# Up block 0 of the next group computed ahead of the down blocks, and seven block products in 120 chunks instead of 78

## The reference

```
h = rmsnorm(x, norm_mix[l]);  proj = h @ w_in[l]
o_a = dsa_branch(...);  o_b = swa_branch(...)          # both add a relative-position bias
merged = sigmoid(h Wg_A) * (o_a @ w_branch_a[l]) + sigmoid(h Wg_B) * (o_b @ w_branch_b[l])
x = x + merged @ w_out[l]
h = rmsnorm(x, norm_mlp[l])
x = x + jnp.square(jax.nn.relu(h @ w_up[l])) @ w_down[l]
```

## Time and profile before

| | |
|---|---|
| median of three runs | 2711.16 us |
| the profiled execution | 2718.1 us, its span 2716.4 us |
| PE busy | 2696.5 us, 99% of the span, 12756 instructions |
| DVE busy | 1768.3 us, 65% |
| ACT busy | 1365.0 us, 50% |
| DMA queue q1 (weights, spread, moved) | 568.67 MB, 64% of 16 engines |
| granted TensorE clock, mean | 0.998 of full speed |

### The profile page before, as it was taken

The page is one execution under the profiler, slowest core; times in us unless marked ns, Lnnn a source line. Parts: engine busy times, 40 slices in busy tenths (PEclk is TensorE's granted clock), DMA queues, the critical chain, the costliest instruction groups (busy, mean ns, idle before and its releaser), DMA issues.

```text
span 2716.4 us, 35283 instructions
## 1 busy us (share of the span) xinstructions
PE 2696.5 (99%) x12756; PEld 2212.7 (81%) x12756; DVE 1768.3 (65%) x2538; ACT 1365.0 (50%) x1735; POOL 21.0 (1%) x29
## 2 busy tenths in 40 slices
PE   9999999999999999999999999999999999999998
PEld 7788778888888887888887887788888888888886
DVE  5565555556686785876656655555666957769665
ACT  5445554445554555545445455544455545455443
POOL 0000000000000000000000000000000000000000
PEclk9999999999999999999999999999999999999999
DMA  7875545676766666667666655566776666676664
GB/s 240 249 229 164 185 155 186 219 230 232 235 215 210 228 199 229 205 218 238 225 219 217 212 171 179 160 202 219 229 251 230 199 223 222 203 231 210 216 226 154
DMA packets 189697, 574.76 MB, mean 212 GB/s; under 512 B 21432, under 2 KB 56856, under 8 KB 189408
## 3 DMA queue, kind: packets, MB, share of 16 engines
q1 hardware_dynamic: 188000, 568.67, 64.0%
q0 software_dynamic: 1152, 3.80, 0.7%
q10 hardware_dynamic: 384, 0.11, 0.0%
HBM read 533.57 MB, written 38.93 MB: 211 GB/s over the span
## 4 chain that ended last, share of the span: by engine, by line
PE 94%; DMA 2%; DVE 1%; issue 1%; ACT 0%; SPq 0%; ACTq 0%; POOLq 0%; POOL 0%; DVEq 0%
PE acc L444 28%; PE acc L445 28%; PE acc L446 28%; DMA scratch<-spread 1%; PE acc L412 1%; PE acc L413 1%; PE acc L414 1%; PE att L412 1%; PE att L414 1%; PE att L413 1%; DMA moved<-scratch 1%; PE turn L413 0%; PE turn L414 0%; PE turn L412 0%; PE att L502 0%
## 5 line engine op out<-in xcount | busy, mean ns | idle before, releaser
L1095 DVE TENSOR_TENSOR w_lo<-raw,w_hi 128x1024 fp32r<-128x1024 f32 (+1 forms) x866 | 1040.9, 1213 | 598.0 <-ACT w_hi L742 596.3
L742 ACT ACTIVATE w_hi<-raw 128x1024 fp32r<-128x1024 f32 (+1 forms) x866 | 903.3, 1051 | 747.3 <-PE acc L446 688.4
L444 PE MATMUL acc<-w_hi,h_hl 128*128 128x512 f32 x2176 | 866.9, 398 | 2.6 <-DVE w_lo L1095 2.1
L446 PE MATMUL acc<-w_hi,h_hl 128*128 128x512 f32 x2176 | 859.3, 395 | 0.0
L445 PE MATMUL acc<-w_lo,h_hl 128*128 128x512 f32 x2176 | 859.1, 395 | 0.0
L444 PEld LDWEIGHTS acc<-w_hi,h_hl 128*128 128x128 f32 x2176 | 409.9, 188 | 105.2 <-DVE w_lo L1095 5.7
L446 PEld LDWEIGHTS acc<-w_hi,h_hl 128*128 128x128 f32 x2176 | 409.8, 188 | 96.9
L445 PEld LDWEIGHTS acc<-w_lo,h_hl 128*128 128x128 f32 x2176 | 410.1, 188 | 94.1
L444 PE MATMUL acc<-w_hi,o_hl 128*128 128x512 f32 x1064 | 421.5, 396 | 0.3 <-DVE o_hl L1193 0.2
L445 PE MATMUL acc<-w_lo,o_hl 128*128 128x512 f32 x1064 | 420.0, 395 | 0.0
L446 PE MATMUL acc<-w_hi,o_hl 128*128 128x512 f32 x1064 | 419.8, 395 | 0.0
(11 more groups left out here) (215 smaller groups left out, 2155.7 us busy)
## 6 DMA issues: line engine op xcount, KB each, us to landing
raw<-in_w_main SPq DMA_DIRECT2D x928, 512.0 KB, 4.2
scratch<-spread SPq DMA_DIRECT2D x67, 512.0 KB, 2.7
moved<-scratch SPq DMA_DIRECT2D x268, 128.0 KB, 3.4
raw<-in_w_misc SPq DMA_DIRECT2D x16, 336.0 KB, 4.8
xs<-in_x SPq DMA_DIRECT2D x4, 512.0 KB, 7.2
out<-xs SPq DMA_DIRECT2D x8, 256.0 KB, 3.1
bias_b<-bias_rows POOLq DMA_DIRECT2D x4, 384.0 KB, 8.2
bias_rows<-probs POOLq DMA_DIRECT2D x2, 576.0 KB, 10.8
```

The source lines that it names most:

```text
L444: nc.tensor.matmul(o, a_hi, hi[:, kk], start=(k == 0), stop=False)
L446: last = nc.tensor.matmul(o, a_lo, hi[:, kk], start=False, stop=fin)
L742: nc.scalar.activation(w_hi[s][:, 0:2 * width], raw[r][:, 0:2 * width], ACT.Copy).then_inc(hi_ready, 1)
L1095: nc.vector.tensor_tensor(w_lo[s][:, 0:2 * width], raw[r][:, 0:2 * width], w_hi[s][:, 0:2 * width].bitcast(F32), ALU.subtract).then_inc(lo ...
```

## The change

1. **Order in the MLP.** Up units 0 and 1 stand ahead of the loop. The loop now runs over U2, U3, V0, D0, D1, D2, D3, V1, where V0 and V1 are up units 0 and 1 of the next group. V0's block of u waits in `moved` until D3 is done.
2. **Seven products in up units.** Chunks 1, 3, 5 of U2 and of V0 (`WIDE_UP`), and of the last group's U2. Of the down chunks 13 in each looped group stay, in D0 at chunks 3 and 7 instead of 1 and 3. That makes 19 a loop turn and 60 a layer, 120 in all. The up form needs sums of blocks of h, made in three of the four `out` units (`sums_of_h`, `h_sums`, kept in `s_hh`).
3. **How such an up block is taken.** ScalarE copies half of one side bank to `stage` (`take_side`), VectorE makes the sum in five operations (`add_up_sides`), at chunk 3; relu and square follow out of `stage`, and the transpose into `spread` comes at chunk 4, behind the split of chunk 3.
4. **Moved blocks later.** `u_moved` and its sums come at chunks 1 and 2 of the next unit instead of chunks 6 and 7 (V0's at chunks 3 and 4 of V1).
5. **Bias.** `COPIES` 8 instead of 32: one store of 288 KB, then 16 reads of 64 KB (`bias_a`) and 16 of 96 KB (`bias_b`), waited for in pairs. `s_hh` has the room of `bias_b`, so `bias_b` is read again for layer 1, during the last group of layer 0.

```diff
-COPIES = 32
+COPIES = 8
-WIDE = ((1, 3), (1, 3, 5, 7), (1, 3, 5), (1, 3, 5, 7))
+WIDE_UP = ((1, 3, 5), (), (1, 3, 5), ())
+WIDE = ((3, 7), (1, 3, 5, 7), (1, 3, 5), (1, 3, 5, 7))
@@ SyncE
-                    for n in range(1, NBLK):
-                        load_up(g, n)
+                    load_up(g, 2, pass_on(l, E_U + 1, g))
+                    load_up(g, 3, pass_on(l, E_U + 2, g))
+                    load_unit(l, g * 64 + (C_MLP + 32), 8, pass_on(l, E_U + 3, g), g * 64 + (C_MLP + 64))
                     for n in range(NBLK):
-                        load_down(g, n)
-                    load_up(g + 1, 0)
+                        load_unit(l, g * 64 + (C_MLP + 40 + 8 * n), 8, pass_on(l, E_U + 4, g) if n == 0 else None,
+                                  g * 64 + (C_MLP + 32 + 8 * n))
+                    load_unit(l, g * 64 + (C_MLP + 72), 8)
@@ ScalarE
+                def take_side(g, n, end):
+                    unit_done(end)
+                    act.wait_ge(spread_ready, g * NBLK + (l * MOVES + E_U + n))
+                    nc.scalar.activation(stage[:, 0, HALF:NB], wide_acc[n % NBLK // 2][0][:, HALF:NB], ACT.Copy)\
+                        .then_inc(sides_out, 1)
+                def take_summed(g, n, count):
+                    act.wait_ge(up_summed, count)
+                    for t in range(TT):
+                        last = nc.scalar.activation(stage[:, t, :], stage[:, t, :], ACT.Relu, scale=rms[:, 0, t:t + 1])
+                    last.then_inc(relued, 1)
+                    square_u(g, n)
@@ VectorE (ScalarE's order is the same with its own halves of the jobs)
+                def add_up_sides(g, n, i):
...
+                    dve.wait_ge(sides_out, at + 1)
+                    nc.vector.tensor_tensor(side_sum, z[:, 0:HALF], quarters[:, 1, :], ALU.add).then_inc(up_step, 1)
+                    dve.wait_ge(up_step, steps + 1)
+                    nc.vector.tensor_tensor(quarters[:, 0::3, :], side_sum.unsqueeze(1).to_broadcast([P, 2, HALF]),
+                                            w[:].rearrange("p (h c) -> p h c", h=2), ALU.subtract).then_inc(up_step, 1)
+                    dve.wait_ge(up_step, steps + 2)
+                    nc.vector.tensor_tensor(quarters[:, 2, :], quarters[:, 3, :], w[:, 0:HALF], ALU.subtract).then_inc(up_step, 1)
+                    nc.vector.tensor_tensor(stage[:, 0, :], acc[0][0][:], stage[:, 0, :], ALU.add)
+                    dve.wait_ge(up_step, steps + 3)
+                    nc.vector.tensor_tensor(stage[:, 1, :], acc[0][1][:], stage[:, 1, :], ALU.add).then_inc(up_summed, 1)
                 with dve.Fori(0, GROUPS - 1) as g:
+                    run(g * 64 + (C_MLP + 16), {3: lambda: spread_u(g, 1)}, (), WIDE_UP[2], steps_at(g, AT_UP2))
+                    run(g * 64 + (C_MLP + 24), {3: lambda: add_up_sides(g, 2, 0), 4: lambda: spread_u(g, 2)},
+                        {1: lambda: u_moved(g, 1), 2: lambda: u_sums_lo(g, 1)})
+                    run(g * 64 + (C_MLP + 32), {3: lambda: spread_u(g, 3)},
+                        {1: lambda: u_moved(g, 2), 2: lambda: u_sums_lo(g, 2)}, WIDE_UP[0], steps_at(g, AT_UP0))
+                    run(g * 64 + (C_MLP + 40), {3: lambda: add_up_sides(g, 0, 1), 4: lambda: spread_u(g, 4)},
+                        {1: lambda: u_moved(g, 3), 2: lambda: u_sums_lo(g, 3)}, WIDE[0], steps_at(g, WIDE_AT[0]))
                     for n in range(1, NBLK):
+                        run(g * 64 + (C_MLP + 40 + 8 * n), {3: lambda n=n: take_down(g, n - 1, g * 64 + (base + 40 + 8 * n))}, (),
+                            WIDE[n], steps_at(g, WIDE_AT[n]))
+                    run(g * 64 + (C_MLP + 72), {3: first_block}, {4: lambda: u_sums_lo(g, 4)})
```

More of the change, by code:

```diff
@@ L358, in _ @@
             pool.wait_ge(rows_out, 1)
[L359 to L363, removed]
+            pool.dma_start(bass.AP(bias_rows.tensor, 0, [[SKEW, ROWS], [REL + 1, COPIES], [1, REL]]),
+                           rows.unsqueeze(1).to_broadcast([ROWS, COPIES, REL])).then_inc(bias_stored, 16)
+            pool.wait_ge(bias_stored, 16)
             for i in range(BIAS_PIECES):
@@ new lines, in adds, with up_two_before, up @@
+                def adds(g, count):
+                    return lambda: pe.wait_ge(dve_took, g * 4 + (l * DVE_UNITS + 13 + count))
+                def up_two_before(g):
+                    def before():
+                        acts(g, 1)()
+                        adds(g, 0)()
+                    return before
+                def up(at, bank, before, n, hold=(), wide=()):
+                    unit(l * CHUNKS + at, 8, h_lhs, acc[bank], None, before, hold=hold, wide=wide, sum_of=h_sum,
+                         sides=wide_acc[n // 2])
@@ new lines, in down, with u_took, u_sums_took @@
+                def down(at, bank, before, n, hold=(), wide=()):
+                    unit(l * CHUNKS + at, 8, o_lhs, acc[bank], None, before, hold=hold, wide=wide, sum_of=u_sum,
+                         sides=wide_acc[1 - n % 2])
+                def u_took(g, n):
+                    return g * NBLK + took_of(E_U + n)
+                def u_sums_took(g, n):
+                    return g * NBLK + (l * U_SUMS + n + 1)
+                up(C_MLP, 0, adds(0, -1), 0, [(0, moved_took, took_of(E_XO + 2)), (6, moved_took, took_of(E_XO + 3))])
@@ L735, in _ @@
+                if l < DEPTH - 1:
+                    down(last + 56, 1, adds(GROUPS - 1, 2), 3)
+                else:
+                    last_unit(l * CHUNKS + last + 56, o_lhs, acc[1], adds(GROUPS - 1, 2))
         @block.scalar
@@ L1056, in down @@
-                    unit(l * CHUNKS + g * 64 + (C_MLP + 32 + 8 * n), 8, take=take, taken=taken, sums=sums,
-                         wide=() if last_group else WIDE[n],
-                         steps=lambda i: g * (3 * N_WIDE) + (l * (GROUPS - 1) * 3 * N_WIDE + 3 * (WIDE_AT[n] + i + 1)))
-                up(0, 0)
-                with act.Fori(0, GROUPS - 1) as g:
-                    for n in range(1, NBLK):
-                        up(g, n)
-                    for n in range(NBLK):
-                        down(g, n)
-                    up(g + 1, 0)
@@ L1579, in _, with take_down, steps_at, run @@
-                up(0, 0)
+                def take_down(g, n, end):
+                    dve.wait_ge(multiplied, end + SLOTS)
+                    take_sides(n)
+                    add_to_x(end, n, bank=1 - n % 2)
+                def steps_at(g, first):
+                    return lambda i: g * (3 * N_WIDE) + 3 * (l * LAYER_WIDE + first + i)
+                def run(at_chunk, at=(), then=(), wide=(), steps=None):
+                    unit(l * CHUNKS + at_chunk, 8, at=at, then=then, wide=wide, steps=steps)
```

409 lines of the change are left out of this document (222 added, 187 removed).

## The result

| | median of runs, us | lowest to highest | profiled execution |
|---|---|---|---|
| before | 2710.48 (4 runs) | 2709.55 to 2712.44 | 2718.1 |
| changed | 2732.89 (4 runs) | 2731.34 to 2735.0 | 2735.0 |

The changed kernel is slower: ratio 1.0082 (1.0065 to 1.0100). Repeated on another chip (five runs of it beside nine of the kernel before) it was 1.0055 (1.0041 to 1.0069).

A forecast was written before the change was run, and what follows sets the result against it. TensorE, busy 99% of the span, was taken as the bound. 2718.1 - 12.6 - 0.7 - 1 + 28.8 = 2732.6 us profiled, or 2711.2 + 14.5 = 2725.7 by the median: forecast 2726, slower, 8-in-10 range 2694 to 2744.

The forecast's parts named there:

- The gain, 42 x 0.30 = 12.6 us: TensorE in the MLP: 42 more chunks take 2.48 instead of 2.78 us, 12.6 us less.
- The late store: U3: U2's block is summed before relu, square and transpose, so its store is 3.2 us later and V0's loads late.
- V0, 9.6 us: V0 in six loop turns: TensorE waits 0.3 at chunk 2, 1.1 at 3, 0.2 at 4, 1.6 us a turn.
- D1, 17.4 us: D1 in six turns: waits of 1.7 us at its start, 1.0 at chunk 3, 0.2 at chunk 4; 2.9 a turn.
- D0, 1.8 us: D0 in six turns: TensorE waits 0.3 us a turn, at chunk 4.
- 28.8 us in the loop: V0, D0 and D1 together: 4.8 us of waits a turn, three turns in each of two layers; bounds 0 and 54.
- Sums of h, last group, second read of `bias_b`: 0, at worst 1: `out` units, last group and second bias read: hidden beside plain chunks, 0; the sums of h at worst 1 us.
- The bias, 1 us gained: Bias traffic: 0.86 MB less stored, same 2.5 MB of reads in smaller pieces; between 3 gained and 3 lost, 1 gained.
- Sum: Whole kernel: 2718.1 - 12.6 - 0.7 - 1 + 28.8 = 2732.6 us profiled; 14.5 added to the median 2711.2.
- only D1 waits: Rival: V0 just makes it and D1 waits 0.9 + 1.2 us, 12.6 in six turns; 2710 us, no change; chance 0.15.
- the cover holds: Rival: stores land early or sums overlap the copies, so the lead never runs out; 2697 us; chance 0.30.
- the third rival: Waits grow: some stores land late, or D1's wait lowers TensorE's clock; 2736 us, late stores up to 2750; chance 0.10.

The follow-up runs named there:

- later take: Changed kernel with relu, square and transpose of U2's block at chunk 6 of U3 instead of 4; 2743.0 us, ratio 1.0112 to before.
- plain chunk 1: Changed kernel with chunk 1 of V0 and D1 no longer in seven products, 108 wide chunks; 2711.3 us, ratio 0.9992 to before.
- loads ahead of the fetch: Changed kernel with SyncE issuing the next unit's loads of chunks 0 and 1 before the moved block's fetch; 2721.4 us, ratio 1.0031 to before.
- `bias_b` later: Changed kernel with bias_b's second read begun behind the root of layer 1's mixing; two runs, 2725.8 and 2724.9 us, ratios 1.0045 and 1.0041 to before.
- order and bias: Changed kernel without seven-product up chunks, `WIDE_UP` empty and U3's take one step again; 2710.1 us, ratio 0.9997 to before.
- the last kernel: Changed kernel with next loads before the fetch, D0 wide at 1 and 5, bias_b read later, D1's chunk 3 plain; 2702.5 us, ratio 0.9965 to before.

## Why the prediction was right, point by point

- *The gain, 42 x 0.30 = 12.6 us.* Held. A chunk of seven products in an up unit takes 2.48 us without a wait, like the one in a down unit, where a plain one takes 2.79. The rule of the Trainium skill that was weighed there (TensorEngine Tiling, Instruction Overhead) would have left 3 us; by the trace 21 products of 256 columns take 2.48 us and 12 of 512 take 2.79, so no such overhead is paid beyond the distance of starts here.
- *The late store.* Held. The store of U2's block comes 7.5 to 8.0 us into U3 in the twelve turns of both profiles, where such a store came at 4.2 before (7.3 forecast for the end of the transpose). In the D0 shown the store (9.70 for 9.9) and the loads (14.58 for 14.5) held to 0.2 us, and the load was there 1.0 us sooner (19.9 for 20.9); in layer 1 D0's store is 1 to 2 us later than forecast. The later take confirmed the direction of the cost, though it cost half of what I expected; the plain chunk 1 and the loads ahead of the fetch showed where it falls.
- *V0, 9.6 us.* Measured 11.0 and 10.7, and at the chunks forecast: 0 to 1.3 us at chunk 2 (0.3 forecast), 1.0 to 1.2 at chunk 3 (1.1), 0.2 at chunk 4 (0.2).
- *D1, 17.4 us.* Measured 12.4 and 11.6. The load came 1.0 us sooner in the turn shown, and the 1.7 us at chunk 0 were 0.6 to 1.1 in the first profile and 0 to 1.4 in the second. Chunk 3 waits 0.8 to 0.9 us (1.0 forecast).
- *D0, 1.8 us.* This step was too small: 10.2 and 7.6. Two things were left out: the store of U3's block landed after 4 to 5.6 us in layer 1, where the prediction had such a landing only as a bound, 4.7 instead of 2.6; and the weight sums of D0's chunk 7 hang on the one load that is issued behind D0's own late store. With the early loads, moving the wide chunks to 1 and 5 took them away from both places, and D0's waits went from 12.7 to 5.0, though that store still took 4.7 to 4.9 us in layer 1.
- *28.8 us in the loop.* 33.6 and 29.9 measured. That the sum came out so well is in part luck: D0 was too low by 6 to 8 and D1 too high by 5 to 6.
- *Sums of h, last group, second read of `bias_b`: 0, at worst 1.* Too small. The rest of the MLP has 6.6 us in the first profile and 4.1 in the second: 2.3 and 1.5 beside the read of `bias_b`, 0.7 in each layer for the last group's U2 at chunks 5 and 6, and in the first profile alone 1.6 of lower clock. Outside the MLP the first profile has 2.3 us more, where the sums of h stand ahead of a split in layer 0's last `out` unit. VectorE and TensorE there:

```profile
644.28 2.19 DVE L1277 SCALAR_TENSOR_TENSOR h_hl<-moved,gain,h_hl 128x128 fp32r<-128x128 f32 x8 [5.80 <-ACT h_hl L862]
646.39 0.28 DVE L1551 TENSOR_SCALAR stage<-moved,gain 128x128 f32<-128x128 f32 x1
...
648.14 1.22 DVE L1166 TENSOR_TENSOR w_lo<-raw,w_hi 128x1024 fp32r<-128x1024 f32 x1
```

```profile
646.83 0.40 PE L475 MATMUL acc<-w_hi,m_hl 128*128 128x512 f32 x1
649.41 0.50 PE L473 MATMUL acc<-w_hi,m_hl 128*128 128x512 f32 x1 [2.19 <-DVE w_lo L1166]
```

The block's store took 5.5 us to land (630.89 to the fetch at 636.41), and the sums, 1.75 us of VectorE (646.39 to 648.14), came on top of that. In the second profile the store took 4.5 us and TensorE did not wait there.

In the last group's U2 VectorE adds the first down block's gathered side sums (`rest`) into `xs` right ahead of the wide split; the prediction had no step for it:

```profile
1238.94 0.42 DVE L1613 TENSOR_TENSOR qk<-qk 128x256 f32<-128x256 f32 x1
...
1240.65 1.23 DVE L1617 TENSOR_TENSOR xs<-xs,qk 128x1024 f32<-128x1024 f32 x1
1241.91 2.03 DVE L1187 TENSOR_TENSOR w_lo<-raw,w_hi 128x1792 fp32r<-128x1792 f32 x1
```

- *The bias, 1 us gained.* 2.7 us by the runs (0.3 to 5.2).
- *Sum.* +14.5 forecast; +22.4 in the first comparison, +15.6 in the second.

Of the rivals, that only D1 waits and that the cover holds are out: V0 and D0 wait in every turn. The waits grew in part as the third rival said: stores landed late, in one place of layer 1. Its other half, the clock, came once in the first profile, not in D1 but behind the wait in the `out` unit. The columns are those of the earlier trace rows:

```profile
650.40:653.84 3.44, 3.44 (x9) 2.64 (x8) 2.97 (x3) 1.33 (x2) 0.00 (x0) 0.51 0.83 246
```

At the lower of its two levels, 1.2 GHz, TensorE starts these products 0.43 us apart instead of 0.23; the mean grant of 0.999 hides it. In all waits of the loop, 1.6 us and shorter in both profiles, the clock held. Of the other profiles with the new order three have such a fall in mid-kernel, each in the last group's D0 of layer 0 at a wait for the moved block: take later (2.4 us of wait), chunk 1 plain (3.1), next loads first (4.7). A wait of 2.7 us in the second run of `bias_b` later had none.

What stays open is why the store of U3's block takes longer to land in layer 1 (4.0 to 5.6 us in six turns of two profiles) than in layer 0 (2.8 to 3.2). The same instructions stand around it in both. Of the twelve kernels and repeats with the new order nine have it late there (3.9 us or more), and three do not: order and bias (2.6), chunk 1 plain (3.1), and the last kernel, with D1's chunk 3 plain (2.8 to 2.9).

## What to carry to other kernels

A change that makes TensorE's part of a unit shorter must be charged with what its new steps put in front of the store, and then followed through the queue that store shares with the next unit's loads: here 42 chunks paid 12.6 us and 30 to 34 us came back in the loop as waits of under 2 us each, none of which any engine's share of busy time shows. Where two such causes sit in series, taking one away may gain nothing (ratio 1.0076, where the changed kernel had 1.0055 beside it) while both together gain over 20 us (0.9976), so a fix that failed alone is not yet refuted. Issue first what the next unit's head needs, and put the heavy chunks where their operands do not come from the transfer that has just been made late.

## What the runs showed that I had not expected

- A fetch may be issued only when its store has landed, and this took 2.6 to 3.2 us in most turns of the MLP. It took 4.0 to 5.6 for one place in layer 1 of the changed kernel, up to 5.5 in the `out` units and up to 4.1 in the MLP's first units. Beside the 96 KB reads of `bias_b` it took 4.2 to 4.4 in the first profile and 3.4 to 6.8 in the second, and 2.7 to 3.0 in both profiles in which these were moved. These 16 reads move 1.5 MB of the kernel's 576, and in the first profile a store beside them took some 1.5 us longer.
- The changed kernel differed between two chips by 5 us (2732.9 and 2728.0), while the kernel before stayed within 2 beside it (2710.5 and 2712.4) and within 2.5 over all four comparisons. It may be that waits which hang on DMA landings repeat less well than a kernel bound by TensorE; two comparisons do not show it.
